# GpSimd applies the norm weights and the output gate to the linear-attention rows while the softmax attention runs

## The reference, cut to what matters

```
h = rms_norm(x, norm1_g);  p = h @ w_in
# four heads of gated linear attention, forward and backward scans summed
o = rms_norm(o_f + o_b, norm_g)            # per head, over its 128 values
a = o.reshape(T, 512) * silu(og)           # the output gate
# four heads of differential softmax attention
w = softmax(s1) - lam * softmax(s2)
d = rms_norm(w @ v, diff_norm_g) * (1 - lam_init)
x = x + concat(a, d) @ w_out
```

## Time and profile before

| what | us |
| --- | --- |
| median of 3 runs | 1631.16 |
| lowest of them | 1629.38 |
| profiled execution, its own time | 1630.23 |
| profiled execution, span from first to last instruction | 1628.4 |
| DVE busy in the span | 1258.4 (77%) |
| ACT busy | 1053.9 (65%) |
| POOL busy | 130.1 (8%) |
| softmax attention, first to last maximum | 300.15 to 377.34 |

### The profile page before, as it was taken

The page is one execution under the profiler, slowest core; times in us unless marked ns, Lnnn a source line. Parts: engine busy times, 40 slices in busy tenths (PEclk is TensorE's granted clock), DMA queues, the critical chain, the costliest instruction groups (busy, mean ns, idle before and its releaser), DMA issues.

```text
span 1628.4 us, 18264 instructions
## 1 busy us (share of the span) xinstructions
PE 1526.7 (94%) x7244; PEld 1113.2 (68%) x7244; DVE 1258.4 (77%) x1137; ACT 1053.9 (65%) x1070; POOL 130.1 (8%) x95
## 2 busy tenths in 40 slices
PE   5999999766994999999999999999999999999996
PEld 4787777445882777777777777777777777777774
DVE  5259586487437889888898888988889888888884
ACT  6434232575213777777777787777877878778774
POOL 1023122000000010100000000000000101000000
PEclk9999999898996999999999999999999999999999
DMA  6111011300138999999999999999999999999991
GB/s 235 53 52 52 1 53 53 142 1 3 78 119 292 374 365 379 374 394 373 378 387 360 395 369 388 376 367 395 374 384 374 377 384 365 392 380 376 381 368 56
DMA packets 192004, 448.58 MB, mean 275 GB/s; under 512 B 12688, under 2 KB 13232, under 8 KB 191920
## 3 DMA queue, kind: packets, MB, share of 16 engines
q1 hardware_dynamic: 187440, 433.16, 71.8%
q0 software_dynamic: 3904, 12.62, 3.4%
q10 hardware_dynamic: 576, 1.64, 0.3%
HBM read 434.80 MB, written 12.58 MB: 275 GB/s over the span
## 4 chain that ended last, share of the span: by engine, by line
PE 83%; DVE 7%; issue 5%; ACT 2%; DMA 1%; POOL 0%; POOLq 0%; SPq 0%; DVEq 0%; ACTq 0%
PE ps L781 21%; PE ps L779 21%; PE ps L780 21%; PE ps L518 5%; PE ps L519 5%; PE ps L520 5%; PE ps L812 1%; DVE st L1397 1%; PE ps L718 1%; DVE states L1243 1%; DMA slice_raw<-in_w_in 1%; PE ps L706 1%; PE ps L772 1%; DVE t L1258 1%; PE ps L698 1%
## 5 line engine op out<-in xcount | busy, mean ns | idle before, releaser
L1543 DVE TENSOR_TENSOR wl<-raw,wh 128x2048 fp32r<-128x2048 f32 x384 | 875.1, 2292 | 142.2 <-ACT wh L1103 137.0
L1103 ACT CAST wh<-raw 128x2048 fp32r<-128x2048 f32 x384 | 730.7, 1912 | 133.7 <-PE ps L781 132.6
L779 PE MATMUL ps<-wh,XTh 128*96 128x512 f32 x1024 | 407.3, 398 | 1.2 <-DVE XTl L1548 1.2
L781 PE MATMUL ps<-wl,XTh 128*96 128x512 f32 x1024 | 405.1, 396 | 0.0
L780 PE MATMUL ps<-wh,XTl 128*96 128x512 f32 x1024 | 402.2, 393 | 0.0
L781 PEld LDWEIGHTS ps<-wl,XTh 128*96 128x96 f32 x1024 | 165.0, 161 | 72.3
L780 PEld LDWEIGHTS ps<-wh,XTl 128*96 128x96 f32 x1024 | 166.0, 162 | 68.6
L779 PEld LDWEIGHTS ps<-wh,XTh 128*96 128x96 f32 x1024 | 165.5, 162 | 68.2 <-DVE XTl L1548 1.5
L779 PE MATMUL ps<-wh,gTh 128*96 128x512 f32 x512 | 201.9, 394 | 1.2 <-DVE gTl L1554 1.2
L781 PE MATMUL ps<-wl,gTh 128*96 128x512 f32 x512 | 201.1, 393 | 0.0
L780 PE MATMUL ps<-wh,gTl 128*96 128x512 f32 x512 | 200.7, 392 | 0.0
(11 more groups left out here) (220 smaller groups left out, 1446.5 us busy)
## 6 DMA issues: line engine op xcount, KB each, us to landing
raw<-in_w_gate SPq DMA_DIRECT2D x128, 1024.0 KB, 8.7
raw<-in_w_up SPq DMA_DIRECT2D x128, 1024.0 KB, 8.8
raw<-in_w_down SPq DMA_DIRECT2D x128, 1024.0 KB, 9.1
slice_raw<-in_w_in SPq DMA_DIRECT2D x6, 2048.0 KB, 9.2
X<-in_x_sample SPq DMA_DIRECT2D x8, 512.0 KB, 10.4
slice_raw<-in_w_out SPq DMA_DIRECT2D x2, 2048.0 KB, 10.6
X<-in_x_prompt SPq DMA_DIRECT2D x4, 512.0 KB, 4.9
h_rows<-hn SPq DMA_DIRECT2D x4, 512.0 KB, 2.7
```

The source lines that it names most:

```text
L779: pe.matmul(out, hi, rhs_h, start=first, stop=False)
L781: return pe.matmul(out, hi, rhs_l, start=False, stop=last)
L1103: act.copy(wh[:, n % CONV, :], raw[:, n % RAW, :]).then_inc(s_wh, 1)
L1543: dve.tensor_tensor(wl[:, n % CONV, :], raw[:, n % RAW, :], wh[:, n % CONV, :].bitcast(F32), ALU.subtract).then_inc(s_wl, 1)
```

## The change

For the linear-attention rows, `head_gain` and `head_gate` leave DVE's `beside`; squares and sums stay. POOL gets a new loop, between its last rotary product and its wait for the normed rows: for every row tile it waits for the squares (a new semaphore `s_sq0` that DVE raises), multiplies the 128 x 512 rows by the norm weights, waits for itself, multiplies them by the gate, and raises the new semaphore `s_og` at each. DVE's wait for the silu values moves to POOL. DVE's wait on its own squares now goes by `s_sq0` where it went by the chain semaphore. `scale_heads(t)` gets a wait until POOL has done both products of row tile t. The softmax rows `OD` are treated as before.

```diff
@@ gpsimd, behind the rotary products, ahead of the waits for the stored rows
+            pool.wait_ge(s_ego, 1)
+            for t in range(NT):
+                gains_of = og_gain[:, 0, :].unsqueeze(1).broadcast_to([P, HEADS, DV])
+                pool.wait_ge(s_sq0, t + 1)
+                pool.tensor_tensor(OA[:, :, t, :], OA[:, :, t, :], gains_of, ALU.mult).then_inc(s_og, 1)
+                pool.wait_ge(s_og, 2 * t + 1)
+                pool.tensor_tensor(OA[:, :, t, :], OA[:, :, t, :],
+                                   OG[:, t, :].rearrange("p (h c) -> p h c", h=HEADS), ALU.mult).then_inc(s_og, 1)
@@ vector
-            def head_gate(m, t):
-                ch.own()
-                ch.mark(dve.tensor_tensor(rows(m, t), rows(m, t), heads(OG[:, t, :]), ALU.mult))
-
             def beside(i):
 
                 if i == 0:
                     dve.wait_ge(s_oc, 2 * HEADS)
-                    dve.wait_ge(s_ego, 1)
-                if i < 4 * NT:
+                if i < 4 * NT and i % 4 < 2:
                     t = i // 4
-                    ch.own()
-                    (head_squares, head_sums, head_gain, head_gate)[i % 4](0, t)
+                    if i % 4 == 0:
+                        ch.own()
+                        dve.tensor_tensor(heads(square[0][:]), rows(0, t), rows(0, t), ALU.mult).then_inc(s_sq0, 1)
+                        dve.wait_ge(s_sq0, t + 1)
+                    else:
+                        head_sums(0, t)
                 if i >= 8 and (i - 8) % 4 == 0:
@@ vector, scale_heads
             def scale_heads(t):
+                dve.wait_ge(s_og, 2 * t + 2)
                 for m in range(2):
```

More of the change, by code:

```diff
@@ L278, in build @@
         s_out = sem("residual_stored")
+        s_sq0, s_og = sem("gla_rows_squared"), sem("gla_rows_gained_and_gated")
         s_issued = sem("first_gather_issued")
@@ L1473, in _ @@
                     dve.wait_ge(s_wr, 32)
-                    dve.tensor_tensor(wr[:], wr[:], gcol[:].unsqueeze(2).broadcast_to([P, KD, NE]), ALU.mult)\
-                        .then_inc(s_wrg, 1)
+                    dve.tensor_tensor(wr[:], wr[:], gcol[:].unsqueeze(2).broadcast_to([P, KD, NE]), ALU.mult)                        .then_inc(s_wrg, 1)
                 if t >= 2:
```

## The result

The changed kernel takes 1633.34 us (median of 19 runs) against 1630.63 for the kernel before (19 runs): ratio 1.0014, interval 1.0008 to 1.0020, which is 2.3 us more (1.3 to 3.3). Repeated later as an experiment it came out at 1.0004 (0.9995 to 1.0013). By 2% that is no change. In the first measurement it is a little slower, beyond its own noise; the second by itself can't tell it from no change. The profiled execution took 1632.78 us with a span of 1631.0, against 1630.23 and 1628.4.

What follows compares the result with a forecast made beforehand. In the softmax attention, DVE bounds the 7.96 us pair of maxima, the loop over PE and ACT the 6.57 us pair. 1630.2 - 0.6 + 2.3 + 0.5 = 1632.4 us; range 1628 to 1638.5.

Steps and rivals of the forecast that it cites:

- The removed work stood where the loop bounds: Softmax attention: twelve DVE instructions removed from the 6.57 us pair of maxima, bound by PE and ACT, gain only 0.6 us.
- GpSimd's product: 1.29: Each 128x512 product on POOL in the attention was to take 1.29 us, between measured 256-wide and 768-wide ones.
- DVE's squares start first: Sample row tiles: DVE's squares of `OD` start before POOL's norm weights, which are held about 0.5 us.
- The rival of 1637.7: POOL's norm weights start ahead of the squares of `OD`, costing 1.9 us in each of four row tiles; chance 0.15.
- The price of a sample row tile: 0.57: Row tiles 2 to 5: DVE's norm weights of `OD` start 0.57 us late behind POOL's product, 2.3 us in all.
- The 0.4 that I worked out from the row of line 439: Alternative price per sample row tile, about 0.4 us, by a POOL product that was blocked for less than a full block.
- Row tile 0: 0.5: DVE's one-column product in row tile 0 waits 0.5 us for POOL's norm weights, delaying the next maxima: +0.5 us.
- Row tile 1: covered: The same 0.5 us stop in row tile 1 costs nothing, covered by a wait of 0.46 us.
- The sum: Whole kernel: 1630.2 - 0.6 + 2.3 + 0.5 = 1632.4 us.
- PE's clock: Rival: one drop of PE's granted clock more or less, 1.6 us to either side; chance 0.05 that it outweighs the rest.

Runs made afterwards that it cites:

- e1: Kernel before with norm weights and gate of the linear-attention rows left out on DVE and GpSimd: 1630.13 us, ratio 0.9998.
- e2: Kernel before, plus two GpSimd products of the same shapes per row tile on an unused spare tile: 1636.32 us, 5.0 over the kernel before.
- e5: Kernel before, DVE alone, softmax rows' squares moved one unit later, their sums and norm weights two units later: 1627.87 us, ratio 0.9978.
- e6: Kernel before, linear norm weights and gate on GpSimd, released by squares and sums; softmax squares two units later, sums and norm weights three: 1623.86 us, ratio 0.9952.
- e8: e6 run once more, unchanged: 1624.40 us, ratio 0.9957 against the kernel before.
- e7: e6 with GpSimd's two products left out, so linear norm weights and gate are missing: 1622.59 us, ratio 0.9951.
- e3: Changed kernel with GpSimd's two products released by DVE's sums, one unit later, instead of by the squares: 1629.11 us, ratio 0.9988.

## Why the prediction was right

It said 1632.4 us, 2.2 over the profiled execution before, in a range from 1628.0 to 1638.5; measured were 1633.34 and, as a ratio, 2.3 us more. The mechanism was the one forecast, and the terms measure so:

- **The removed work stood where the loop bounds.** Right, and shown by e1: the twelve instructions are worth 0.6 us in one place, and the sample's pairs of maxima without a drop of the clock kept their lengths (7.97, and 6.56 for 6.57).
- **GpSimd's product: 1.29.** 1.27 alone. Right.
- **DVE's squares start first.** Right, 0.04 to 0.05 us ahead, in both traces; they stayed at 0.69. The rival of 1637.7, in which GpSimd starts first, fell with this.
- **The price of a sample row tile: 0.57.** Right in kind, too large in size: the pairs with squares are 0.34 to 0.38 longer. I let the squares hold the operands for their pitch of 0.61; GpSimd's product shows 0.50 of stop (1.776 less 1.27); a full block to the end of DVE's row would have been 0.65 (0.69 less the 0.04 that DVE was ahead), and it was not that. And a DVE instruction seems to get its operands some 0.1 us before the end that GpSimd's row shows: 326.05 + 1.77 = 327.82, but the held norm weights, at 327.34 with 0.36 of delay, must have been running by 327.70 if they then took their usual time. The 0.4 that I worked out from the row of line 439 was the better price. The four tiles cost 1.5, not 2.3.
- **Row tile 0: 0.5.** 0.43: the one-column product took 0.59 instead of 0.16.
- **Row tile 1: covered.** This step failed, for two reasons. I took 0.3 us for GpSimd's wait for itself, from a fill followed by a transfer; between two products it is 0.07. And I took DVE's one-column product where the trace before has it, 1.52 us behind the start of the squares; in the changed kernel's traces it is due 2.14 and 2.21 behind. So the gate came 0.04 us ahead of it and held it for a whole product (0.11 ahead in the second trace):

```profile
314.05 1.27 POOL L492 TENSOR_TENSOR OA<-OA,og_gain 128x512 f32<-128x512 f32 x1 [6.67 <-DVE square L1383]
315.39 1.27 POOL L494 TENSOR_TENSOR OA<-OA,OG 128x512 f32<-128x512 f32 x1
...
315.43 1.24 DVE L1415 TENSOR_TENSOR st<-st,nlam 128x1 f32<-128x1 f32 x1
```

  The product is late because the maximum of unit 6 is, and that because PE did unit 6's scores at the lower of its two clocks, 1.2 GHz (a granted clock of 0.50 from 314.40 to 315.70 in the second trace of the changed kernel). Here are these scores in the trace before, and in the changed kernel's first trace with the maximum behind them; the scores end at 314.53, and that is what the maximum waited for, though the view names DVE:

```profile
315.00 0.70 PE L676 MATMUL ps<-KT,QT 64*128 64x256 f32 x4
```

```profile
313.37 1.16 PE L686 MATMUL ps<-KT,QT 64*128 64x256 f32 x4
...
314.63 0.69 DVE L1406 TENSOR_REDUCE st<-ps 128x2 f32<-128x512 f32 x1 [0.67 <-DVE square L1383]
```

  The scores of unit 6 are slow in seven of the twelve traces, the second of the kernel before among them, so the edit is not needed for it. With fast scores the product would be due while GpSimd's norm weights run, as the prediction had it; no trace of the changed kernel shows that case.

  From the maximum of unit 6 to that of unit 8 it is 4.51 in both traces of the kernel before, 4.88 in the second trace of the changed one and 4.99 in e2: +0.4, not 0. (In the first trace of the changed kernel it is 6.46, with the clock down.)
- **The sum** with measured terms: -0.6 + 1.5 + 0.4 + 0.4 = +1.7 us, within the 1.3 to 3.3 measured and near its lower end. Too much in one term and too little in another partly cancelled, so the closeness of 2.2 to 2.3 is in part luck; the second measurement of the changed kernel gave 0.7.
- **PE's clock.** I gave a drop more or less 1.6 us, and that size is seen (pairs of 8.18 for 6.57), as are smaller and larger ones (7.4 to 8.8). But it isn't a coin thrown once: two traces of the kernel before differ by 1.9 us in the attention through it, and it fell least in the kernels with the spread order (0.99 and 1.00 in e5, e6 and e8, but 0.97 in e7, no more than in e3). That is an association of a dozen traces, not a test. Part of the 7.8 us of e6 is this clock. By the pitches, its four pairs with squares take 26.1 instead of 31.6, 5.5 less; the three others, at 6.7, take 0.4 more than undisturbed ones of 6.57; the gate of row tile 1 gives 0.6. That makes 5.7, less the 0.4 of row tile 0, so 5.3; the rest is in the drops of the kernel before, whose other pairs go up to between 7.5 and 8.8, and which e6 doesn't have.

## What to carry to other kernels

Moving work to an idle engine gains only if the work stood on the path: look where the engine it leaves has waits, not how busy it is, and move the work out of the stretch without waits. In a software pipeline of alternating heavy and light steps, two moves belong together: here removing work from the light steps alone gave 0.6 us (e1), levelling the steps alone 1.4 by its pitches (e5), and both together 5.3 (e6). An engine with spare time can still slow its neighbour through shared operands; then the time at which it is released, a unit sooner or later, decides between a loss, nothing and a gain.

## What the runs showed of the hardware that was not expected

A DVE instruction on one column (0.16 us) is held like a long one when it reads two SBUF operands while GpSimd reads: it took 1.24 and 1.25 us. Who gets the operands was decided by 0.04 us, both ways round: DVE's squares at 326.01 ahead of GpSimd at 326.05, and GpSimd's gate at 315.39 ahead of DVE at 315.43. Instructions that read one operand from PSUM (the maxima, 1.21) or one from SBUF (the sums, 0.68) were not held, and fills of GpSimd held neither of the two groups that its products hold. And two executions of the same kernel differ by 2 us in the attention alone, and 1.2 of that stands in one pair of maxima (8.78 for 7.54) whose length goes with PE's granted clock.
